# Modulation rows on ScalarE's queue, all rounded copies on ScalarE, another placing of the expert rows, and unread products on TensorE in the first pass

## What is computed

```python
# first block
proj = rmsnorm(x) @ w_in                        # 12 chunks of 256 columns
x += rmsnorm(concat(rms(forgetting_attention), rms(chunked_relpos_attention)) @ w_out)
x += rmsnorm(memory_cross_attention(rmsnorm(x), mem))
x += rmsnorm(square(relu(rmsnorm(x) @ w_ff1)) @ w_ff2)
# second block
mod = silu(c) @ w_ada + b_ada                   # 6 x 1024 numbers for all tokens
h = rms_norm(x) * (1 + scale1) + shift1
x += gate1 * (concat(sliding_window(h), rms(gla(h)) * silu(gg)) @ w_out_2)
h2 = rms_norm(x) * (1 + scale2) + shift2
# per token: 8 heads x 16 best of 16384 experts, rows of u and v gathered from HBM
hid = gelu(u[expert] . h2) * gates
x += gate2 * sum(hid * v[expert])
return rms_norm(x)
```

## Time and profile before

| | us |
|---|---|
| median of 3 runs | 3083.5 (3074.08 to 3090.07) |
| the profiled execution | 3080.89 |
| its span | 3079.2 |
| mean granted TensorE clock | 0.882 |
| busy: TensorE, VectorE, GpSimd, ScalarE | 2407.3, 1799.2, 1487.6, 801.0 |

### The profile page before, as it was taken

The page is one execution under the profiler, slowest core; times in us unless marked ns, Lnnn a source line. Parts: engine busy times, 40 slices in busy tenths (PEclk is TensorE's granted clock), DMA queues, the critical chain, the costliest instruction groups (busy, mean ns, idle before and its releaser), DMA issues.

```text
span 3079.2 us, 33119 instructions
## 1 busy us (share of the span) xinstructions
PE 2407.3 (78%) x11936; PEld 1694.9 (55%) x11936; DVE 1799.2 (58%) x3817; ACT 801.0 (26%) x1748; POOL 1487.6 (48%) x1239
## 2 busy tenths in 40 slices
PE   7998745456887789979999999899667776667676
PEld 7867745456867675657787866567222222222222
DVE  5444444445664876576765677665765466654444
ACT  2132300000242232343533345333211112121111
POOL 5613222224412331145544455364877777777764
PEclk9958877778858895589999999899999999999998
DMA  5513334344413563478999998597999999999997
GB/s 183 173 53 117 109 129 141 133 138 161 137 35 106 163 229 122 137 265 310 339 331 346 337 342 316 197 351 273 351 345 354 370 348 360 357 351 371 365 349 265
DMA packets 228579, 758.89 MB, mean 246 GB/s; under 512 B 23985, under 2 KB 49601, under 8 KB 227522
## 3 DMA queue, kind: packets, MB, share of 16 engines
q0 software_dynamic: 147456, 536.94, 48.3%
q1 hardware_dynamic: 80962, 219.85, 20.9%
HBM read 751.97 MB, written 4.72 MB: 246 GB/s over the span
## 4 chain that ended last, share of the span: by engine, by line
PE 43%; POOL 21%; DVE 15%; DMA 10%; issue 8%; ACT 2%; another core or an unknown queue 1%; SPq 0%; DVEq 0%; POOLq 0%; ACTq 0%
POOL rings L524 10%; POOL rings L516 10%; PE bank L1266 8%; PE bank L921 8%; PE bank L923 8%; PE bank L922 8%; DMA weights<-in_w_ff 6%; PE bank L1024 3%; DVE weights_split L1296 2%; DMA rings<-in_peer_v,scratch 2%; DVE area L1439 1%; DVE rings L1739 1%; PE bank L1007 1%; DVE weights_split L1299 1%; PE bank L991 1%
## 5 line engine op out<-in xcount | busy, mean ns | idle before, releaser
L1266 PE MATMUL bank<-rings,weight_diagonals 128*128 128x512 f32 x1944 | 957.9, 625 | 293.5 <-DMA rings<-in_peer_v,scratch 225.7
L1266 PEld LDWEIGHTS bank<-rings,weight_diagonals 128*128 128x128 f32 x1944 | 350.1, 196 | 832.5 <-issue 668.1
L1739 DVE CUSTOM_DVE_ANT_0 rings<-rings,token_rows 128x1024 f32<-128x1024 f32 x512 | 617.2, 1223 | 316.4 <-DMA rings<-in_peer_u,scratch 283.4
L524 POOL DMA_INDIRECT rings<-in_peer_v,scratch x512 | 573.7, 1120 | 471.1 <-PE bank L1266 320.6
L516 POOL DMA_INDIRECT rings<-in_peer_u,scratch x512 | 590.8, 1154 | 400.6 <-DVE scratch L1739 247.3
L921 PE MATMUL bank<-h_T_high,weights_split 128*128 128x256 f32 (+1 forms) x1376 | 422.5, 307 | 146.0 <-POOL weights_split L467 106.7
L466 POOL CAST weights_split<-weights 128x1024 fp32r<-128x1024 f32 x86 | 95.4, 1109 | 693.6 <-DMA weights<-in_w_ff 314.2
L1299 DVE TENSOR_TENSOR weights_split<-weights,weights_split 128x1024 fp32r<-128x1024 f32 x242 | 300.0, 1250 | 207.7 <-ACT weights_split L549 161.0
L922 PE MATMUL bank<-h_T_low,weights_split 128*128 128x256 f32 (+1 forms) x1376 | 405.3, 295 | 0.0
L923 PE MATMUL bank<-h_T_high,weights_split 128*128 128x256 f32 (+1 forms) x1376 | 404.5, 294 | 0.0
L877 ACT ACTIVATE weight_diagonals<-ident,scratch 128x128 f32<-128x128 f32 x486 | 190.3, 400 | 767.6 <-PE bank L1266 448.6
(11 more groups left out here) (319 smaller groups left out, 3197.6 us busy)
## 6 DMA issues: line engine op xcount, KB each, us to landing
weights<-in_w_ff SPq DMA_DIRECT2D x128, 512.0 KB
weights<-in_w_in SPq DMA_DIRECT2D x88, 512.0 KB
area<-in_w_ada SPq DMA_DIRECT2D x48, 512.0 KB, 4.7
weights<-in_w_out SPq DMA_DIRECT2D x32, 512.0 KB
weights<-in_w_pq SPq DMA_DIRECT2D x32, 512.0 KB
weights<-in_w_mq SPq DMA_DIRECT2D x16, 512.0 KB
weights<-in_w_mo SPq DMA_DIRECT2D x16, 512.0 KB
rings<-in_peer_u,scratch POOLq DMA_INDIRECT x512
```

Of the source, the lines that this page charges most:

```text
L524: pool.indirect_dma_start(vring[k], None, A["peer_v"], index(n)).then_inc(v_landed[k], 16)
L1266: ins = pe.matmul(bank[half][:], wdiag[:, i % 4, :], vring[d % RV][:, half * COLS:(half + 1) * COLS], start=(r == 0), stop=(r == SLOTS - 1))
L1739: dve.tensor_tensor_reduce(out=uring[k], in0=uring[k], in1=token[:, b % 2, :], scale=1.0, scalar=0.0, op0=ALU.mult, op1=ALU.add, accum_out ...
```

## The change

- All rounded copies of pass 0 are made by ScalarE too; GpSimd and VectorE only make the differences.
- The modulation rows are loaded from ScalarE's queue (`modulations`): two at the start of the feed-forward, then two at the end of each of its steps 0 to 22. VectorE uses a pair at the beginning of each step from step 0, before it splits the next chunk's half.
- `mark` takes another list of planned durations with the number of weight chunks of each stage; a stage gets (us - 2.9 x chunks) / 2.76 rows. Within pass 1 this makes 211 rows.
- `busy(p, n)` issues n bf16 products of 128 x 128 by 512 columns into a bank that nobody reads then, in pass 0 only: 24 before the transposes of seven turns and 8 after them (not for `N_MEM` and `N_MIX`), and 2 in each step of the attentions between the transposes and the products with the values.
- The load of the last gain row moves from before chunk `out2` 0 to before `wq` 0 of pass 1.

```diff
-ROWS_WITHIN = 232
+STAGES = [("mixn", 1, 14, 0), ("in", 12, 82, 12), ("fox", 20, 46, 0), ("chk", 20, 46, 0), ("y", 1, 11, 0), ("out", 4, 26, 4), ("post0", 1, 12, 0),
+          ("memn", 1, 4, 0), ("mq", 4, 25, 4), ("mem", 12, 16, 0), ("memy", 1, 7, 0), ("mo", 4, 26, 4), ("post1", 1, 12, 0), ("ffn", 1, 4, 0),
+          ("ff", 32, 200, 32), ("post2", 1, 12, 0), ("attn", 1, 6, 0), ("in2", 10, 66, 10), ("swa", 20, 36, 0), ("gla", 10, 44, 0), ("mixed", 1, 8, 0),
+          ("out2", 4, 26, 4), ("add", 1, 12, 0), ("peern", 1, 6, 0), ("wq", 8, 64, 8)]
+CHUNK_US, ROW_US = 2.9, 2.76
...
-                if p == 0 and name in ("f1", "f2"):
-                    for r in range(rows, min(48, 2 * (c - ORD[0, "f1", 0] - 1))):
-                        if r >= 2:
-                            sp.wait_ge(ada_used, r - 1)
-                        sp.dma_start(ada[:, r % 2, :], A["w_ada"][r]).then_inc(ada_landed[r % 2], 16)
-                        rows = r + 1
...
-                if key == (1, "out2", 0):
+                if key == (1, "wq", 0):
...
             def split(c):
-                pool.wait_ge(w_landed[w % W_SLOTS], 16 * (w // W_SLOTS + 1))
-                link(pool.tensor_copy(high, raw))
+                pool.wait_ge(w_high, w + 1)
                 pool.tensor_tensor(low, raw, high.bitcast(F32), ALU.subtract).then_inc(w_split_pool, 1)
...
-            fed = [2 * FIRST[1]]
+            fed = [0]
...
+            def modulations(lo, hi):
+                for r in range(lo, hi):
+                    if r >= 2:
+                        act.wait_ge(ada_used, r - 1)
+                    act.dma_start(ada[:, r % 2, :], A["w_ada"][r]).then_inc(ada_landed[r % 2], 16)
...
                     act.activation(crow, crow, ACT.Silu).then_inc(c_ready, 1)
+                    modulations(0, 2)
...
+                    if p == 0 and t < 23:
+                        modulations(2 * t + 2, 2 * t + 4)
...
+            def busy(p, n):
+                if p == 0:
+                    for _ in range(n):
+                        pe.matmul(bank[0], identb[:], onesb[:], start=True, stop=True)
...
             def turned(p, n, src, signal, value):
+                if n not in (N_MEM, N_MIX):
+                    busy(p, 24)
...
+                if n not in (N_MEM, N_MIX):
+                    busy(p, 8)
...
                         turn(u - 3)
+                    busy(p, 2)
...
-                    if w < 2 * FIRST[1]:
-                        if w % 2 == 0:
-                            continue
-                        dve.wait_ge(w_landed[w % W_SLOTS], 16 * (w // W_SLOTS + 1))
-                        link(dve.tensor_copy(high, raw))
-                    else:
-                        dve.wait_ge(w_high, w - 2 * FIRST[1] + 1)
+                    if w < 2 * FIRST[1] and w % 2 == 0:
+                        continue
+                    dve.wait_ge(w_high, w + 1)
```

More of the change, by code:

```diff
@@ L124, in unit @@
     return "swa", (u - U_SWA) // 2, u % 2, (P if 2 * p + u % 2 == 0 else 2 * P)
-STAGES = [("mixn", 1, 10), ("in", 12, 70), ("fox", 20, 42), ("chk", 20, 38), ("y", 1, 9), ("out", 4, 23), ("post0", 1, 10),
-          ("memn", 1, 5), ("mq", 4, 23), ("mem", 12, 22), ("memy", 1, 5), ("mo", 4, 23), ("post1", 1, 10), ("ffn", 1, 5),
-          ("ff", 32, 186), ("post2", 1, 10), ("attn", 1, 6), ("in2", 10, 60), ("swa", 20, 28), ("gla", 10, 45), ("mixed", 1, 6),
-          ("out2", 4, 23), ("add", 1, 5), ("peern", 1, 8), ("wq", 8, 53)]
-LENGTH = sum(us for _, _, us in STAGES)
-ROWS_WITHIN = 232
+STAGES = [("mixn", 1, 14, 0), ("in", 12, 82, 12), ("fox", 20, 46, 0), ("chk", 20, 46, 0), ("y", 1, 11, 0), ("out", 4, 26, 4), ("post0", 1, 12, 0),
[3 more added lines that the diff above has]
+CHUNK_US, ROW_US = 2.9, 2.76
 def mark(stage, i=0):
     at = 0.0
-    for name, n, us in STAGES:
+    for name, n, us, chunks in STAGES:
+        rows = (us - CHUNK_US * chunks) / ROW_US
         if name == stage:
-            return int((at + us * (i + 1) / n) * ROWS_WITHIN / LENGTH)
-        at += us
+            return int(at + rows * (i + 1) / n)
+        at += rows
     raise ValueError(stage)
@@ L374, in rest @@
                     sp.dma_start(X[:, b, :], A["x"][b]).then_inc(x_landed[b], 16)
-            rows = 0
             for c, (p, name, i) in enumerate(ORDER):
@@ L641, in work @@
                         squares(N_MIX, b, X[:, b, :])
+                    feed(ORD[p, "mk", 0])
                     turned(p, N_MEM)
@@ L1599, in work @@
                 for t, (kind, f) in enumerate(FF_ORDER):
+                    if p == 0:
+                        if t == 0:
+                            dve.wait_ge(c_ready, 1)
+                        if t < 24:
+                            modulate(2 * t)
+                            modulate(2 * t + 1)
+                        if t == 24:
+                            modulated()
                     feed(ORD[p, kind, f] + 1)
@@ L1602, in work @@
                         hidden_split(p, f)
-                    if p == 0:
-                        if t == 1:
-                            dve.wait_ge(c_ready, 1)
-                        if 1 <= t < 25:
-                            modulate(2 * t - 2)
-                            modulate(2 * t - 1)
-                        if t == 26:
-                            modulated()
                     if t == 31:
```

## The result

The kernel after takes **2927.8 us** (median of 4 runs, 2922.4 to 2947.1) against 3078.8 us for the kernel before beside it (3069.8 to 3090.1): a ratio of 0.952, with a 95% interval of 0.946 to 0.958. Faster, as forecast, and inside the range; but 45 us above the forecast of 2883. The profiled execution spans 2920.6 us against 3079.2, so 158.6 us less where the sum said 200.

The account below looks back on a forecast made before the run. Bounded by an order: SyncE's wait for VectorE before modulation rows held back weight loads in pass 0's feed-forward. -187 - 3 - 5 - 24 + 19 = -200 on 3080.9 gave 2881, 2883 us at the median; range 2838 to 2975.

Parts of the forecast that it names:

- main case: Whole kernel: all five terms come as priced, 2883 us, own range 2840 to 2915, chance 0.55.
- term 5: Expert rows re-placed, 211 within pass 1 instead of 232: plus 19 us (minus 5 to plus 35).
- terms 2 to 4: Pass 0: rounded copies on ScalarE, minus 3; unread products at the turns, minus 5, and in attention units, minus 24.
- term 1: Pass 0's feed-forward: modulation rows on ScalarE's queue free the weight loads, 7.5 us a chunk, minus 187 us.
- rival C: Pass 0's feed-forward: the moved modulation rows save issue time only, minus 35 instead of minus 187; 3034 us, chance 0.02.
- Rival B: Pass 0's feed-forward: slow landings make the loop 9.1 us or a little more; 2919 to 2935 us, chance 0.10.
- Rival A: Fox, chk and swa of pass 0: clock stays low despite unread products, term 4 (these products) plus 45; 2972 us, chance 0.23.
- F: Pass 0's feed-forward: the modulation rows' queue did not hold the weights, so term 1 vanishes; 3069 us, chance 0.02.

Follow-up runs that it names:

- e2: The kernel after without any unread products; 0.949 of the kernel before.
- e8: The kernel after with pass 0's rounded copies back on GpSimd and VectorE, modulation rows still on ScalarE's queue; 0.960 of the kernel before.
- e4: The kernel after with modulation rows back on SyncE's queue and VectorE's old order, rounded copies still on ScalarE; 1.004 of the kernel before.
- e1: The kernel after with the old placing of expert rows, 232 within pass 1; 0.930 of the kernel before.
- e5: The kernel after run again unchanged, on another chip; 2929.5 us, 0.950 of the kernel before.
- e9: The kernel after with the old placing of expert rows, 232 within pass 1, on another chip; 0.933 of the kernel before.
- e12: The kernel after with some six expert rows moved from swa and gla of pass 1 into its feed-forward, 211 rows kept; 0.944 of the kernel before.
- e3: The kernel after with the old list of row places but 211 rows within pass 1; 0.946 of the kernel before.
- e10: e7 with the load of the last gain row back before chunk out2 0; 0.926 of the kernel before.
- e7: e6 without the unread products in memory attention and before its transposes; 0.927 of the kernel before.
- e6: The kernel after with the old row placing and two unread products per unit in fox and chk of pass 1 too; 0.930 of the kernel before.
- e11: e10 with four unread products instead of two per unit in fox and chk of pass 1; 2840.7 us, 0.923 of the kernel before.

## Why the prediction was right, and where it was off

The direction and the range were right, and so was the main case as a mechanism: the freed queue and the raised clock brought the gain. But the result lies 13 us outside the main case's own range, which reached to 2915, and the sum is 41 us off on the profiles because term 5 missed by 31 and terms 2 to 4 by 19, with 9 us more from term 1 on the other side. Term by term, on the profiled executions:

**1. Modulation rows on ScalarE's queue: forecast minus 187, measured minus 196** (413.4 to 217.5). The loop was forecast at 7.5 us a chunk with a landing of 5.5; the stage ran at 7.1 (170.6 over 24) with 5.4 in the median. The clock was to be 1.0 and is 0.95; no wait of SyncE for VectorE is left. That the mean is so near is in part luck: the chunks don't come at the even pace of one loop but 5.7 to 11.1 us apart, and ScalarE waits almost as long for weights (36.0 us) as for dot products (47.6). Some 5 of the 196 belong to the products ahead of the stage (e2). One thing in the working I hadn't separated: the copies are part of it. The queue alone brings 168 us (e8), and ScalarE's copies 28 more, because without them VectorE's 6.9 us of work a chunk and its waits would be the loop. The rule of the Trainium skill that spoke against it ("DMA: Bandwidth & Descriptors", section "Issuing engines are not separate DMA queues") would have given 35 us, rival C. The trace doesn't agree with that as the price of the move: e4, which differs from the kernel after in the queue of the rows and in VectorE's order of work alone, takes 181 us longer in this stage (398.6 against 217.5). The rule counts the time to issue; what the move took away was a wait with other transfers queued behind it. Rival B, slow landings, didn't come true either, with more bytes per microsecond than before (295 against 139 GB/s).

**2. Rounded copies outside the feed-forward: forecast minus 3, measured nothing** by itself. The hole of the earlier trace rows shrank from 6.0 to 3.4 us, and another of 2.2 in the first projection, behind GpSimd, took the time.

**3 and 4. Unread products: forecast minus 29 together, measured about minus 13** over all stages of pass 0 but the feed-forward (and 12.9 by e2). This is the second miss, 16 us. The mechanism held: the clock is at 1.00 in fox, chk and swa, as these windows of the kernel after show, with the columns of the earlier trace rows (fox, chk, swa).

```profile
159.00:189.00 30.00, 29.34 (x189) 20.67 (x194) 13.45 (x54) 13.04 (x49) 5.97 (x13) 1.00 0.11 36
190.00:217.00 27.00, 26.84 (x146) 17.80 (x150) 14.38 (x85) 13.41 (x51) 0.00 (x0) 1.00 0.28 79
660.00:690.00 30.00, 28.06 (x159) 18.49 (x164) 18.74 (x84) 16.52 (x66) 0.00 (x0) 1.00 0.06 22
```

Rival A, by which it would stay low and cost 45 us, fell. The pairs' pace, from the timeline of TensorE in fox, two scores two units apart:

```profile
176.09 0.70 PE L1000 MATMUL bank<-area 64*128 64x256 f32 x2
...
179.56 0.70 PE L1000 MATMUL bank<-area 64*128 64x256 f32 x2
```

A pair takes 3.47 us where I had 3.2, in chk 3.09 against 2.9, in swa 3.18 against 3.1: over eight pairs of each some 4 us less gain. TensorE is still 98 to 99% busy in fox and chk, now at full clock, so the products themselves probably lie on the path. Memory attention was priced rightly, at 4 plus 5.3 us, and took 9.2 more. One run of products there, before the turn:

```profile
310.57 5.34 PE L964 MATMUL bank<-ones_bf,ident_bf 128*128 128x512 bf16 x23
...
315.75 1.91 PE L972 MATMUL bank<-ident,x_norm 128*128 128x128 f32 x16
...
317.50 1.89 PE L964 MATMUL bank<-ones_bf,ident_bf 128*128 128x512 bf16 x8
```

24 products last 5.3 us as forecast. What missed was the small change: the quicker first chunks and transposes, forecast at about 14 us over seven turns, show as a few (out minus 1.2, the turn behind it plus 2.0, mo minus 1.4, in2 plus 2.6, out2 minus 1.5, the turn before wq minus 2.9).

**5. Rows re-placed: forecast plus 19 (minus 5 to plus 35), measured plus 52 or more by e1, e5 and e9, and 50 by the two profiles. This is the step that failed**, and the only one known to have left its own bounds. (Its five parts as written add up to plus 18.) Its parts:

- The tail: forecast plus 62 for 21 rows, measured plus 64.5. Right.
- The feed-forward of pass 1: forecast 284 to about 252, measured 249.8; 59 rows to 39 (235 instructions to 155, four a row). Right, 34.4 us, 1.72 a row.
- The other chunk stages, 17 rows fewer: forecast minus 29 by the same price, **measured plus 7** (wq plus 5.8, out plus 4.7, out2 plus 1.9, in2 minus 2.9, mq minus 2.0, mo minus 0.4). The sums of their six windows, each from its first to its last weight product, before and then after, show two things. The rows hadn't lain in idle time: TensorE was idle for 4.4 of 301.3 us before. But its busy time fell by only 7.1 us (the products of expert rows from 212 to 180 in these windows, eight rows and not 17; busy with them 92.7 and 79.0 us), and its idle time grew to 18.8 us: waits for VectorE's differences in out, in2 and out2 (3.0, 3.2, 3.3 us) and one for ScalarE in wq (8.0 us, 2.6 before), with the clock at 0.94 to 0.96 in in2, out2 and wq, where it was 1.00.

```profile
sum 301.30, PE 296.88 PEld 246.04 DVE 191.41 ACT 110.92 POOL 160.14; mean PE 49.48 PEld 41.01 DVE 31.90 ACT 18.49 POOL 26.69
```

```profile
sum 308.60, PE 289.78 PEld 245.68 DVE 178.57 ACT 109.63 POOL 139.24; mean PE 48.30 PEld 40.95 DVE 29.76 ACT 18.27 POOL 23.21
```

- The stages between: forecast plus 20, measured plus 8, of which swa+gla alone took plus 18 when its rows went from 27 to 33, and the others minus 10. The number of rows isn't the whole of it: e12 has 27 rows there too and takes 127.4 us, ten more than the kernel before (117.6), and e3 with 25 rows takes 122.3.
- fox and chk: forecast plus 5, measured plus 11.8.
- The first projection: forecast minus 5, measured minus 5.2.

Groups of VectorE's dot products in fox and chk of pass 1, the kernel after, the one before (its window 1162.5 to 1319.5), then e3 (947.6 to 1114.4):

```profile
L1750 DVE CUSTOM_DVE_ANT_0 rings<-rings,token_rows 128x1024 f32<-128x1024 f32 x38 | 46.1, 1218 | 0.3
```

```profile
L1739 DVE CUSTOM_DVE_ANT_0 rings<-rings,token_rows 128x1024 f32<-128x1024 f32 x29 | 35.3, 1218 | 0.2
```

```profile
L1750 DVE CUSTOM_DVE_ANT_0 rings<-rings,token_rows 128x1024 f32<-128x1024 f32 x26 | 31.7, 1218 | 0.7 <-DVE scratch L1763 0.3 <-issue 0.3
```

Nine more dot products of 1.22 us are 10.8 us, and the stage grew by 11.8, where I had put at most 5. The two numbers agree, but the dot products aren't shown as the cause: e3 has 26 of them in these stages, three fewer than the kernel before and e1, and takes 166.7 us, almost as long as the kernel after with 38 (e1: 158.8). So the number of rows alone doesn't decide it. That their places between the units do is likely, but no run shows it, and the price of a row in an attention stays open.

The step that failed is that I priced a row taken out of any chunk stage as one out of the feed-forward, "37 x 1.72 = minus 64"; the move brought 34 us from one stage and lost 7 in the rest, so that the saving which was to pay for the longer tail fell short by 36. In those stages fewer products left than the formulas had it, and what left turned into waits. Were that price right everywhere, e3 with its 21 rows fewer would have been 36 us shorter in pass 1 than e1 and not 15.5. Both conditions that I named as making me wrong, over 10 us a chunk, or pass 1 and the tail together shorter, stayed away: pass 1 and the tail grew by 50.4 us together.

Sum of what was measured: minus 196, 0, minus 13 and plus 50 are minus 159, the difference of the two spans. Two small things in the recorded working: a product of an expert row, given as 429 ns, comes out of the earlier trace rows and the 5.76 us a chunk at 425 (284.2 less 32 x 5.76, over 235); and by its own sum rivals C and F stand at 3035 and 3070 us, not 3034 and 3069. Nothing hangs on either.

What stays open: why rows in attentions, turns and short chunk stages cost what they cost (the stages that take back the feed-forward's 27 us are listed under e3, their reason isn't known), and what part of term 1 is the queue and what part VectorE's new order.

## What to carry to other kernels

Where a queue waits for a semaphore, look at what is queued behind that wait: it is that, and not the time to issue, which moving the transfer to another engine's queue gives back, up to the next loop, whose mean period could here be worked out from rows beforehand. Work that fills holes has no single price: a row was worth 1.72 us in the long feed-forward; taking rows out of the other chunk stages brought nothing, though TensorE was as busy there; a row cost 1.4 to 3.0 in the attention it was moved into and 2.3 to 3.1 in the tail; measure the price in each stage from which it is taken and to which it goes, and don't move it for the sake of one. Unread products paid where TensorE was nearly always busy at its low clock and they brought the clock up (in one profile, e10, two a unit didn't bring it far enough to pay), and cost their full time where the clock was high already.

## What the runs showed of the hardware

Two unread products of 512 bf16 columns per unit held the granted clock at 1.00 in fox, chk and swa of pass 0, but in fox and chk of pass 1 at 0.70, 0.77 and 0.84 in three kernels (e10, e7, e6), and four at 0.94 (e11). Of TensorE's two levels (1.2 and 2.4 GHz) these are mixtures. What tells the three apart isn't known; they are one profile each, and the executions of e7 alone have mean clocks from 0.944 to 0.957.

A tail of indirect loads, with the DMA engines 93 to 94% busy, takes a different time on another chip: the kernel before 3033.8 us against 3076.9 and 3082.3, and for one and the same kernel (e1, e9) the passes within 4 us and the tail 35 us apart (889.5 and 924.5). Times of two chips should be compared as ratios to a common kernel only, and small differences not even so, since what 21 rows cost in the tail differs too (48.1 us from e1 to e3, 64.5 from before to after).

A float32 difference on VectorE took 2.20 us in e8 (mean of 19) and 1.22 us in the feed-forward of the kernel after. It isn't GpSimd's copies alone that go with it: in e4 GpSimd makes none either, and VectorE's difference took 2.23 us where GpSimd's ran at the same time.

```profile
461.51 2.34 POOL L467 TENSOR_TENSOR weights_split<-weights,weights_split 128x1024 fp32r<-128x1024 f32 x1 [13.52 <-ACT weights_split L549]
...
462.70 2.23 DVE L1314 TENSOR_TENSOR weights_split<-weights,weights_split 128x1024 fp32r<-128x1024 f32 x1 [10.02 <-ACT weights_split L549]
```

In the kernel after the one at 394.33 took 1.22 us; GpSimd's had ended at 391.62 and the next began at 395.95. In the first 1000 us of before, after, e4 and e8 no difference that ran with GpSimd idle took more than 1.23 us, and those that met it took 1.2 to 3.3.
